# Sample attention values in a hybrid decoder step: cache pages become the stationary operand and the probabilities of two heads the moving one

## The reference, cut to what matters

```python
# _fox_sample: q (8,1,8,64); k_past, v_past (8,1024,8,64) gathered through page_table
k_all = jnp.concatenate([k_past, k], axis=1)
v_all = jnp.concatenate([v_past, v], axis=1)
c_all = jnp.cumsum(jnp.concatenate([logf_past, logf], axis=1), axis=1)
...
s = jnp.einsum('bqhd,bkhd->bhqk', q, k) * (HEAD_DIM ** -0.5) + (cq - ck)
p = jax.nn.softmax(s, axis=-1)
out = jnp.einsum('bhqk,bkhd->bqhd', p, v)      # what the change is about: p @ v of the samples
# y = concat([out, silu(gr) * head_norm(retention)]) @ w_out
```

## Time and profile before

| what | value |
|---|---|
| time, three runs | 2747.84, 2734.92 and 2734.47 us, median 2734.92 |
| span of the profiled execution | 2743.9 us |
| TensorE busy | 2498.2 us, 91% |
| TensorE weight loads | 2240.8 us, 82% |
| VectorE busy | 918.1 us, 33% |
| ScalarE busy | 846.3 us, 31% |
| GpSimd busy | 1084.8 us, 40% |
| TensorE's mean granted clock | 0.940 of full speed |

### The profile page before, as it was taken

One profiled execution on the slowest core, in us unless ns is written; L12 is line 12 of the kernel. 1 busy time (PEld: TensorE's weight loads), 2 busy tenths in 40 slices (PEclk: granted clock), 3 DMA queues, 4 the chain that ended last, 5 costly groups with the idle time before them and its releaser, 6 DMA issues.

```text
span 2743.9 us, 45520 instructions
## 1 busy us (share of the span) xinstructions
PE 2498.2 (91%) x18440; PEld 2240.8 (82%) x18440; DVE 918.1 (33%) x1069; ACT 846.3 (31%) x1176; POOL 1084.8 (40%) x544
## 2 busy tenths in 40 slices
PE   7999999799889988699999889999979886999996
PEld 2899999679742347599999889999969875999995
DVE  1122202446244445622211442220253456222214
ACT  3222333422212233332232342233333243322213
POOL 1344476424300011344466644447643323444343
PEclk9999999889969988899999989999989997999998
DMA  7233454247313334233355323335412351333321
GB/s 262 63 91 92 124 158 141 75 131 221 102 59 98 114 94 151 65 89 92 92 156 158 94 62 92 92 116 166 141 39 85 101 175 56 96 89 90 94 87 51
DMA packets 448322, 298.44 MB, mean 109 GB/s; under 512 B 20103, under 2 KB 422119, under 8 KB 448087
## 3 DMA queue, kind: packets, MB, share of 16 engines
q1 hardware_dynamic: 448214, 296.92, 36.3%
HBM read 291.36 MB, written 5.53 MB: 108 GB/s over the span
## 4 chain that ended last, share of the span: by engine, by line
PE 57%; DVE 7%; issue 3%; DMA 2%; ACT 2%; POOL 2%; SPq 0%; DVEq 0%; POOLq 0%; ACTq 0%
PE ps L706 45%; PE ps L975 2%; PE ps L728 1%; PE ps L730 1%; PE ps L961 1%; PE ps L965 1%; DMA raw<-w_out_odd 1%; DMA raw<-w_out_even 1%; DVE sq_sum L1588 1%; DVE ada_lo_proj L425 1%; PE ps L1014 1%; DVE ada_lo_h L425 1%; PE ps L1007 1%; DVE rdev L1626 1%; POOL w_lo L656 1%
## 5 line engine op out<-in xcount | busy, mean ns | idle before, releaser
L656 POOL TENSOR_TENSOR w_lo<-raw,w_hi 128x1024 fp32r<-128x1024 f32 (+1 forms) x308 | 802.6, 2607 | 1255.4 <-ACT w_hi L1204 1254.9
L706 PE MATMUL ps<-h_hi,w_hi 128*128 128x260 f32 x3584 | 730.0, 285 | 25.3 <-POOL w_lo L656 15.9
L706 PE MATMUL ps<-h_hi,w_lo 128*128 128x260 f32 x3584 | 728.5, 285 | 0.0
L706 PE MATMUL ps<-h_lo,w_hi 128*128 128x260 f32 x3584 | 728.3, 285 | 0.0
L1204 ACT ACTIVATE w_hi<-raw 128x1024 fp32r<-128x1024 f32 (+1 forms) x308 | 346.6, 1126 | 1233.4 <-PE ps L706 1121.3
L706 PEld LDWEIGHTS ps<-h_hi,w_hi 128*128 128x128 f32 x3584 | 560.0, 191 | 30.4 <-POOL w_lo L656 13.2
L706 PEld LDWEIGHTS ps<-h_hi,w_lo 128*128 128x128 f32 x3584 | 559.6, 191 | 0.0
L706 PEld LDWEIGHTS ps<-h_lo,w_hi 128*128 128x128 f32 x3584 | 558.7, 191 | 0.0
L706 PE MATMUL ps<-hid_hi,w_hi 128*128 128x260 f32 x1408 | 286.6, 285 | 13.8 <-DVE hid_lo L1920 13.8
L706 PE MATMUL ps<-hid_hi,w_lo 128*128 128x260 f32 x1408 | 284.9, 284 | 0.0
L706 PE MATMUL ps<-hid_lo,w_hi 128*128 128x260 f32 x1408 | 284.2, 284 | 0.0
(11 more groups left out here) (296 smaller groups left out, 2375.8 us busy)
## 6 DMA issues: line engine op xcount, KB each, us to landing
raw<-w_ffn_in SPq DMA_DIRECT2D x176, 512.0 KB, 3.7
ada_w<-w_ada SPq DMA_DIRECT2D x120, 512.0 KB, 4.4
raw<-w_ffn_out SPq DMA_DIRECT2D x64, 704.0 KB, 4.4
pages<-cache_k SPq DMA_DIRECT2D x64, 256.0 KB, 3.0
pages<-cache_v SPq DMA_DIRECT2D x64, 256.0 KB, 3.0
raw<-w_in_even SPq DMA_DIRECT2D x28, 512.0 KB, 4.1
raw<-w_in_odd SPq DMA_DIRECT2D x24, 512.0 KB, 3.7
ada_first<-w_ada SPq DMA_DIRECT2D x5, 2048.0 KB, 14.3
```

The costliest lines, as they stand in the source:

```text
L656: pool.tensor_tensor(w_lo[:, k, 0:kt, :], raw[:, k, 0:kt, :], w_hi[:, k, 0:kt, :].bitcast(F32), ALU.subtract).then_inc(chunk_cut, 1)
L706: mm = pe.matmul(ps[:, 2 * q + half, 0:HT], w[:, k, t, :], v[:, kt0 + t, half, :], start=start and t == 0 and step == 0, stop=stop and t = ...
```

## The change

`page_values` swaps the sides. Each page is now the stationary operand in four pieces of 128 tokens by 128 value columns (two heads each), and the moving operand is the two columns of probabilities of those two heads, `s_samp[:, b, 2m:2m+2, g]`. One result is 128 rows (two heads of 64) by 2 columns, and all 8 samples by 4 pieces by 2 columns are gathered in columns 0 to 63 of bank 7. Both matmuls keep full fp32 operands. After the last page two copies by VectorE (`samples_read`) take the upper 64 rows of column u = 0 and the lower 64 rows of column u = 1 into `fox_s`, already in head layout. Masking (`own`, `own_kept`), the eight `unit` matmuls, the addition L1822 and ScalarE's wait for `fox_turned` go; the transposes of `s_prod` now wait for `new_v` only; L1840's copy becomes an addition of `fox_s`. Before the fourth head-mean matmul, which writes bank 7, TensorE waits for `samples_read`.

```diff
@@ build_step @@
-        own_parts = [put(t, [NH, n, FOXW], F32, at) for t, n, at in
-                     (("own_a", 4, R_TOK + 24576), ("own_b", 2, R_H), ("own_c", 2, R_H + 4 * 1280))]
-        own = [part[:, i, :] for part, n in zip(own_parts, (4, 2, 2)) for i in range(n)]
...
@@ -268,6 +262,7 @@
         ret_state = new("ret_state", [128, 4, HD])
         sm = {t: new("sm_" + t, [128, 64]) for t in ("new", "max", "den", "col")}
         eps_gn = new("eps_gn", [128, 1])
+        fox_s = sm["max"][:, 0:32].rearrange("p (m b) -> p m b", m=4)
         PJ = (0, 128, 384, 768)
         AK = (0, 512, 896, 1152)
 
@@ -970,9 +965,11 @@
                     k = g // 4
                     if g % 4 == 0:
                         pe.wait_ge(page_full[k], 64 * (NS + b + 1))
-                    if g == 0 and b:
-                        pe.wait_ge(ev("own_kept"), b)
-                    mm = pe.matmul(ps[0:NH, 7, :], s_samp[:, b, :, g], pages[:, k, g % 4, :], start=g == 0, stop=g == NPG - 1)
+                    for m in range(4):
+                        at = (b * 4 + m) * 2
+                        mm = pe.matmul(ps[:, 7, at:at + 2], pages[:, k, g % 4, m * 128:(m + 1) * 128],
+                                       s_samp[:, b, 2 * m:2 * m + 2, g], start=g == 0 and m == 0, stop=g == NPG - 1,
+                                       skip_group_check=True)
                     if g % 4 == 3:
                         mm.then_inc(ev("v_used"), 1)
 
@@ -1017,6 +1014,8 @@
 
                 pe.wait_ge(ev("o_read"), 8)
                 for m in range(4):
+                    if m == 3:
+                        pe.wait_ge(ev("samples_read"), 2)
                     for half in range(2):
                         mm = pe.matmul(ps[:, 2 * m + half, 0:HT], head_mean, proj[:, VR + m, half * HT:(half + 1) * HT],
                                        start=True, stop=True)
@@ -1030,18 +1029,13 @@
                                        start=m == 0, stop=m == 3)
                     mm.then_inc(ev("hn_var"), 1)
 
-                pe.wait_ge(ev("own_kept"), NS)
-                for b in range(NS):
-                    mm = pe.matmul(ps[0:NS, 2, :], unit[:, b, :], own[b], start=b == 0, stop=b == NS - 1)
-                mm.then_inc(ev("fox_turned"), 1)
-
                 pe.wait_ge(ev("hn_recip"), 1)
                 for m, q in enumerate((2, 3, 0)):
                     for half in range(2):
                         mm = pe.matmul(ps[:, 2 * q + half, 0:HT], from_row[:, m, :], hn_dev[:, half * HT:(half + 1) * HT],
                                        start=True, stop=True)
                     mm.then_inc(ev("hn_spread"), 1)
-                pe.wait_ge(ev("fox_rows"), 1)
+                pe.wait_ge(ev("new_v"), 1)
                 for m in range(4):
                     mm = pe.transpose(ps[:, 3, m * 8:m * 8 + 8], s_prod[:, m * 128:(m + 1) * 128], ident[0:8, 0:8])
                 mm.then_inc(ev("fox_turned"), 1)
@@ -1322,7 +1316,6 @@
                 act.activation(hn_dev[:, :].rearrange("p (h c) -> p h c", h=2), ps[0:NH, 0:2, 0:HT], ACT.Sqrt,
                                bias=eps_gn[0:NH, :]).then_inc(ev("hn_dev_done"), 1)
 
-                act.wait_ge(ev("fox_turned"), 1)
                 for t in range(KT):
                     if t >= 4:
                         act.wait_ge(ev("hn_scaled"), t - 3)
@@ -1795,11 +1788,6 @@
                 for h in range(NH):
                     if h + 1 < NH:
                         masked_scores(h + 1)
-
-                    dve.wait_ge(ev("v_used"), 2 * h + 2)
-                    dve.tensor_tensor(own[h].rearrange("p (h d) -> p h d", h=NH),
-                                      ps[0:NH, 7, :].rearrange("p (h d) -> p h d", h=NH),
-                                      delta[:, :, 0:1].to_broadcast([NH, NH, HD]), ALU.mult).then_inc(ev("own_kept"), 1)
                     if h + 1 < NH:
                         normalise(h + 1)
                     if h % 2:
@@ -1809,6 +1797,11 @@
                         dve.wait_ge(ev("fox_av"), h + 1)
                         dve.tensor_copy(proj[:, VF + m, 0:SEQ], ps[:, 4, :]).then_inc(ev("o_read"), 1)
 
+                dve.wait_ge(ev("v_used"), 2 * NS)
+                by_page = ps[:, 7, 0:64].rearrange("p (b m u) -> p m b u", b=NS, m=4)
+                for u in range(2):
+                    r = slice(64 * u, 64 * u + 64)
+                    dve.tensor_copy(fox_s[r], by_page[r, :, :, u]).then_inc(ev("samples_read"), 1)
                 for m in range(4):
                     tile = proj[:, VR + m]
                     dve.wait_ge(ev("hn_mean"), m + 1)
@@ -1817,10 +1810,6 @@
                 dve.wait_ge(ev("hn_dev_done"), 1)
                 dve.reciprocal(hn_dev[:, :], hn_dev[:, :]).then_inc(ev("hn_recip"), 1)
 
-                dve.wait_ge(ev("fox_turned"), 1)
-                dve.wait_ge(ev("new_v"), 1)
-                dve.tensor_tensor(s_prod[:, :], s_prod[:, :], ps[0:NS, 2, :], ALU.add).then_inc(ev("fox_rows"), 1)
-
                 def low_part(t):
                     dve.wait_ge(ev("cat_hi"), t + 1)
                     dve.tensor_tensor(h_lo[:, t, :, 0:HP], mixed_tile(t)[:, 0:SEQ].rearrange("p (h c) -> p h c", h=2),
@@ -1836,9 +1825,10 @@
                     dve.tensor_tensor(tile.rearrange("p (h c) -> p h c", h=2), tile.rearrange("p (h c) -> p h c", h=2),
                                       pair((2, 3, 0, 2)[m]), ALU.mult).then_inc(ev("hn_scaled"), 1)
                     if m == 1:
-                        dve.wait_ge(ev("fox_turned"), 2)
-                        dve.tensor_copy(proj[:, VF:VF + 4, SEQ:NTOK], ps[:, 3, 0:32].rearrange("p (m b) -> p m b", m=4)
-                                        ).then_inc(ev("fox_s_done"), 1)
+                        dve.wait_ge(ev("fox_turned"), 1)
+                        dve.wait_ge(ev("samples_read"), 2)
+                        dve.tensor_tensor(proj[:, VF:VF + 4, SEQ:NTOK], ps[:, 3, 0:32].rearrange("p (m b) -> p m b", m=4),
+                                          fox_s, ALU.add).then_inc(ev("fox_s_done"), 1)
                 for t in range(2, KT):
                     low_part(t)
                 for u, first in enumerate((VF, VR)):
```

More of the change, by code:

```diff
@@ L97, in host_tables @@
     bd[:64, :64] = bd[64:, 64:] = 1.0 / HD
-    unit = np.zeros((128, 8, 8), f)
-    unit[:, np.arange(8), np.arange(8)] = 1
     two_parts = np.zeros((128, 9), f)
@@ L102, in host_tables @@
     res = np.concatenate([ident, ones, ones / D, p[:, None].astype(f), gdec, tail.reshape(128, 32),
-                          delta.reshape(128, 64), sel.reshape(128, 1024), bd, unit.reshape(128, 64), two_parts], axis=1)
+                          delta.reshape(128, 64), sel.reshape(128, 1024), bd, two_parts], axis=1)
     tri = np.zeros((128, 896), f)
@@ L194, in build_step @@
         dev = sq[:, 0]
-        res = new("res", [128, 1710])
+        res = new("res", [128, 1646])
         ident, ones, mean_w = res[:, 0:128], res[:, 128:256], res[:, 256:384]
@@ L202, in build_step @@
         head_mean = res[:, 1509:1637]
-        two_parts = res[0:18, 1701:1710]
-        unit = res[0:8, 1637:1701].rearrange("p (b c) -> p b c", b=8)
+        two_parts = res[0:18, 1637:1646]
         params = new("params", [128, 4 * 128])
```

## The result

The changed kernel takes 2825.72 us, median of four runs (2822.56 to 2827.8), beside 2741.38 us for the kernel before (four runs, 2734.47 to 2750.23). The ratio is 1.0308, 95% interval 1.0283 to 1.0332: slower by 84 us. Forecast were 2808 us and a range of 2768 to 2836.

The account below looks back on a forecast made before the run. The prediction took TensorE to bound the loop over heads. Loop +78.4 us, mostly from the clock falling in score parts, and tail -5.2 gave +73.2, so 2808 us; range 2768 to 2836.

Parts of the forecast that it names:

- What a page costs: Page matmuls in the loop: 0.98 us against 0.96 at 2.4 GHz, 1.78 against 1.81 at 1.2 GHz; 56 pages, +0.6 us.
- The clock falls and comes back: Loop over heads: clock falls in each score part, returns in each value part; six steps +70.8 us; chance 0.81.
- How fast it falls: Score parts of steps 1 to 6: 3.4 us at the high level before the fall, each part 24.4 us, +9.8.
- the prediction's own factor: Score part at 1.2 GHz against 2.4 GHz: 27.36 us against 14.61, 1.87 times as long.
- The rise: Value parts: the clock returns after 4 us, between 1 and 5.2; each value part +2.0 us.
- Steps 0 and 7: First and last loop steps: step 0 +1.4 us; step 7 +3.6 with its eight pages and +2.0 in its value part.
- The tail: After the loop: with L1035 gone, L1041 starts at the reciprocal's end and everything behind it moves, -5.2 us.
- the 2785 to 2824 that I gave the forecast itself: Whole kernel: narrower range in us for the clock falling and returning each step, from differing fall, rise and pass times.
- The clock stays up: Rival for the loop: loading weights counts for the clock as streaming does; -4.6 us, 2730 us; chance 0.09.
- Never comes back: Rival for the loop: the clock never returns, so value parts are low too; +127, 2861 us; chance 0.05.
- loads don't slow down: Rival for pages at the low clock: a page stays at 0.95 us; 2769 us in all; chance 0.03.
- loads cheaper than any row: Rival for page loads: 0.09 us or less a pass with the clock up; 2720 us, faster; chance 0.02.

Follow-up runs that it names:

- e1_wide120: The changed kernel with 120 columns of probabilities streamed behind each of the 512 page loads instead of 2; 2747.49 us, ratio 1.0024 to the kernel before.
- e3_rows8: The kernel before the change, with each page contracted over 8 of its 128 tokens, 512 columns still streamed; 2831.53 us, ratio 1.0330 to the kernel before.
- e4_tail_only: The kernel before the change without the eight unit matmuls (L1035) and the addition L1822, loop unchanged; 2739.12 us, ratio 0.9991 to the kernel before.
- e5_mixed: As e1_wide120, but the fourth piece of each page streams only its two wanted columns; 2744.90 us, ratio 1.0015 to the kernel before.
- e6_before_front: The kernel before the change, with four pages of step 0 ahead of the spread, the others behind score blocks 1 to 4; 2735.99 us, ratio 0.9969.

## Why the prediction was right, and where its sizes were off

- **What a page costs.** 0.99 us with the clock up and 1.80 with it down, against 0.98 and 1.78 forecast. A 1.80 us slot less the 0.10 us switch, by eight, is 0.21 us a pass. The Trainium skill (TensorE: Matmul & The Clock Gate, section "LDWEIGHTS (loading the stationary operand)") gives a load one price, its columns over 1.2 in ns, by which I estimate 107 ns here. This trace agrees with the clock up and disagrees with it down, and the measurement decides.
- **The clock falls and comes back.** This was the term that decides, and it holds: the score part of step 1 reads 0.50 from 841.6 on. That it is the clock and not the loads is shown by e1_wide120 (same loads, clock up, 0.2% over before) and e3_rows8 (no such loads, clock down, same loss).
- **How fast it falls: mis-sized.** I took 3.4 us at the high level in a score part; it was 841.6 - 839.18 = 2.4 us, under even the shorter of my two bounds, 2.65. By the prediction's own factor, 2.4 + 12.2 x 1.87 = 25.2 us; measured 864.30 - 839.18 = 25.12, forecast 24.4. The nearest fall in the rows came 4.2 us behind the work that brought it; a lag from one place didn't carry over to another, and why the two differ is not shown. The rise took 868.9 - 864.3 = 4.6 us against 4. Six steps gave (1043.65 - 839.18) - (965.53 - 837.38) = +76.3 us against +70.8 and the pages' +0.6.
- **Steps 0 and 7.** Step 0: 35.99 us (803.19 to 839.18) instead of 34.59, +1.4 as forecast. Step 7: 21.28 us (1043.65 to 1064.93) instead of 14.57, +6.7 against +5.6.
- **The tail.** L1035 came 5.17 us nearer to the variance sums, forecast 5.2; from the first head mean to the output projection, at 1093.21, it is 28.28 us instead of 33.73, -5.45. The waits named for it (ScalarE's and VectorE's for L1035) were the ones, and e4_tail_only shows it alone. VectorE's wait of 5.33 us stands in this row of the kernel before, which the earlier trace rows leaves out:

```profile
997.21 0.67 DVE L1822 TENSOR_TENSOR s_prod<-s_prod,ps 8x512 f32<-8x512 f32 x1 [5.33 <-PE ps L1035]
```

- **The sum.** Loop and its start +84.8 (1064.93 - 980.10), tail -5.45, and 2.7 us more behind it, where the change touches nothing: +82.1 in the span against +73.2. The cause of the 2.7 us stays open; it isn't the clock, which in three stretches from the output projection to the end reads 0.94, 0.98 and 0.94, and before 0.94, 0.98 and 0.93. Of the 17.7 us from 2808 to 2825.7, 11.1 are the change (84.3 between the medians against 73.2) and 6.5 the base: I set out from 2734.9 us, and with one more run the median of before is 2741.4.
- **The range.** The result lies inside 2768 to 2836, but just above the 2785 to 2824 that I gave the forecast itself, and the clock's early fall and the low base both pushed it there. The early end of that range is +56 by its own terms and not +58, which moves nothing.
- **The rivals.** *The clock stays up* would have read 1.00 in step 1. The rule beside it (the Trainium skill, TensorE: Matmul & The Clock Gate, section "Why this matters for your kernels", falls tied to idle gaps) doesn't describe these falls: in 841.70:868.80 TensorE is busy for all 27.10 us, and in 839.20:841.60, ahead of the fall, for all 2.40. *Never comes back* is refuted by 1.00 in 869.00:873.20, *loads don't slow down* by the 1.80 us slot, *loads cheaper than any row* by the 0.99.

## What to carry to other kernels

Before an operand is swapped to save streamed columns, look at what keeps the granted clock up around it: here 512 columns through 128 rows, seven eighths of the result thrown away, held the clock up; two wanted columns behind each load took the same time at one clock, and 84 us more by the clock that was lost. Read the granted clock stretch by stretch, and not the engine's busy share, which was 100% in the score part in both cases. Where a stretch is low though TensorE is busy, try to gather the long 128-row streams at its start: putting four pages of step 0 together gave 12 us at that place, and 0.3% of the time, without any new work.

## What was not expected of the hardware

- Streams of 512 columns through 8 rows let the clock fall just as loads with two columns do: steps of 34.13 us in e3_rows8, 34.04 after the change.
- The clock's answer isn't the same in identical steps: 21.43 us or 32.47 us in e5_mixed, with the same instructions on TensorE and in both no gap but the 0.69 us for ScalarE's `p_t`. What sets one step apart from the other stays open.
- The clock came up 2.8 us after the first of four pages that stand together (803.30 to 806.1 in e6_before_front), while in the kernel before the gapless work from 802.79 to 830.15, with the same pages between score blocks, didn't raise it.
